# Norms that take shift and scale as sums in PSUM, with their weights loaded earlier and the split parts written directly

## What is computed

```python
mod = jax.nn.silu(c) @ ada_w[i] + ada_b[i]                  # 6 x 1024 values
sh_a, sc_a, g_a, sh_f, sc_f, g_f = jnp.split(mod[:, None, :], 6, axis=-1)
h = rms_norm(x, attn_norm[i]) * (1.0 + sc_a) + sh_a
x = x + g_a * mixer(h)
h = rms_norm(x, ffn_norm[i]) * (1.0 + sc_f) + sh_f
x = x + g_f * swiglu(h)
```

## Time and profile before

| | |
|---|---|
| median of the runs | 2864.67 us |
| profiled execution | 2865.48 us |
| its span | 2863.7 us |
| PE busy | 2196.3 us (77%) |
| PEld busy | 1930.6 us (67%) |
| DVE busy | 1775.3 us (62%) |
| ACT busy | 903.8 us (32%) |
| POOL busy | 113.3 us (4%) |
| moved by DMA | 368.84 MB, 129 GB/s on average |

### The profile page before, as it was taken

How to read it: one execution, slowest core, us unless ns; L and a number is a source line. 1 busy time by engine, 2 the same in 40 slices (tenths; PEclk the granted TensorE clock), 3 DMA queues, 4 the chain that set the end, 5 groups by cost and what they waited for, 6 DMA issues and landing times. The chain is left out here.

```text
span 2863.7 us, 43489 instructions
## 1 busy us (share of the span) xinstructions
PE 2196.3 (77%) x16766; PEld 1930.6 (67%) x16766; DVE 1775.3 (62%) x2988; ACT 903.8 (32%) x1244; POOL 113.3 (4%) x102
## 2 busy tenths in 40 slices
PE   4936665997844599679778876550679999999997
PEld 2936334996733599467476776550569999999996
DVE  2564226776775677467336668459976666666665
ACT  1300222432323233132322422220554444444443
POOL 0000000000000000043000023000000000000000
PEclk8955557999865799889765988785899999999998
DMA  5635005884702487231100000310025555555554
GB/s 184 221 59 151 0 2 183 320 310 171 258 10 76 160 299 281 74 119 59 59 3 1 5 3 27 138 59 0 0 95 185 183 189 190 184 183 190 189 183 148
DMA packets 153588, 368.84 MB, mean 129 GB/s; under 512 B 10992, under 2 KB 93680, under 8 KB 141296
## 3 DMA queue, kind: packets, MB, share of 16 engines
q1 hardware_dynamic: 153312, 365.93, 36.7%
q10 hardware_dynamic: 144, 1.05, 0.1%
HBM read 364.32 MB, written 2.62 MB: 128 GB/s over the span
## 5 line engine op out<-in xcount | busy, mean ns | idle before, releaser
L981 PE MATMUL experts_pa<-all_h_hi,experts_u_hi 128*128 128x256 f32 x1024 | 290.1, 283 | 7.4 <-DVE experts_u_lo L1052 7.4
L983 PE MATMUL experts_pa<-all_h_hi,experts_u_lo 128*128 128x256 f32 x1024 | 290.5, 284 | 0.0
L982 PE MATMUL experts_pa<-all_h_lo,experts_u_hi 128*128 128x256 f32 x1024 | 290.5, 284 | 0.0
L1228 PE MATMUL ffn_pa<-all_h_hi,ffn_u_hi 128*128 128x256 f32 x704 | 198.6, 282 | 29.6 <-DVE ffn_u_lo L1287 29.6
L1057 DVE TENSOR_TENSOR experts_v_lo<-experts_v,experts_v_hi 128x1024 fp32r<-128x1024 f32 x128 | 156.8, 1225 | 92.1 <-ACT experts_v_hi L1026 92.1
L981 PEld LDWEIGHTS experts_pa<-all_h_hi,experts_u_hi 128*128 128x128 f32 x1024 | 196.9, 192 | 12.5 <-DVE experts_u_lo L1052 7.6
L994 PE MATMUL experts_py<-experts_v_lo,experts_c_hi 128*128 128x512 f32 x512 | 201.0, 393 | 0.0
L982 PEld LDWEIGHTS experts_pa<-all_h_lo,experts_u_hi 128*128 128x128 f32 x1024 | 196.9, 192 | 4.9
L993 PE MATMUL experts_py<-experts_v_hi,experts_c_hi 128*128 128x512 f32 x512 | 200.1, 391 | 0.0
L1229 PE MATMUL ffn_pa<-all_h_lo,ffn_u_hi 128*128 128x256 f32 x704 | 198.1, 281 | 0.0
L1230 PE MATMUL ffn_pa<-all_h_hi,ffn_u_lo 128*128 128x256 f32 x704 | 197.9, 281 | 0.0
(11 more groups left out here) (543 smaller groups left out, 5467.5 us busy)
## 6 DMA issues: line engine op xcount, KB each, us to landing
experts_u<-in_peer_u SPq DMA_DIRECT2D x128, 512.0 KB, 4.4
experts_v<-in_peer_v SPq DMA_DIRECT2D x128, 512.0 KB, 3.3
ffn_u<-in_ffn_columns SPq DMA_DIRECT2D x44, 1024.0 KB, 7.9
ffn_ada_w<-in_ada_w SPq DMA_DIRECT2D x36, 1024.0 KB, 5.4
ffn_v<-in_ffn_rows SPq DMA_DIRECT2D x44, 512.0 KB, 8.1
proj_ada_w<-in_ada_w SPq DMA_DIRECT2D x12, 1024.0 KB, 5.7
proj_w<-in_diff_w_in SPq DMA_DIRECT2D x12, 1024.0 KB, 5.8
main_mod<-in_dn_w_qkv SPq DMA_DIRECT2D x24, 512.0 KB, 3.3
```

What stands on the lines that cost most here:

```text
L981: pe.matmul(out, u_hi[:, b, cols], h_hi[:, c, :], start=(c == 0), stop=False)
L982: pe.matmul(out, u_hi[:, b, cols], h_lo[:, c, :], start=False, stop=False)
L983: last = pe.matmul(out, u_lo[:, b, cols], h_hi[:, c, :], start=False, stop=(c == KT - 1))
L1228: pe.matmul(out, u_hi[:, b, cols], h_hi[:, c, :], start=(c == 0), stop=False)
```

## The change

- The stages `ada0b`, `ada1b`, `ada2b`, the two `split_h` stages and the stage that loads `ctx` are gone.
- A class `Sums` does the same sums inside other stages. For each piece of 512 columns PE does the matmul with ones and a second one, of one row, that adds the bias (loaded to one partition). Four norms (fnorm0, norm1, dnorm, dcnorm) take their scale and shift (4 pieces) directly from PSUM. The other pieces are made by PE and copied to the row by ACT in out0 (4 pieces), rope1 (8) and dnon (8).
- In `normed` the gain comes in an argument and has been loaded in an earlier stage (`constants`, ffn0, ffn1, dnout). The instructions have another order: x times the scaled gain first, and one instruction per half tile for the reciprocal and the shift.
- For norm0, fnorm0, norm1, fnorm1 and pnorm the turned h isn't copied to `h_t`: ACT writes hi from PSUM, and DVE lo. `project` and `peer_scores` then don't split h.

```diff
-def finish_modulation(nc, k, name, bias, rows):
+class Sums:
+    def __init__(self, nc, k, st, row, bias, jobs, banks):
+        self.b = st.sb("sum_b", [1, len(jobs) * CW])
+        self.psum = st.ps("sum_psum", [P, banks, CW])
...
+    def load(self, sp):
...
+            sp.dma_start(self.b[0:1, at * CW:(at + n) * CW],
+                         self.bias[self.jobs[at] * CW:(self.jobs[at] + n) * CW].unsqueeze(0)).then_inc(self.loaded, 16)
...
+    def sum(self, pe):
+        pe.wait_ge(self.loaded, self.loads)
+        for n, j in enumerate(self.jobs):
+            if n >= self.banks:
+                pe.wait_ge(self.moved, n - self.banks + 1)
+            out = self.psum[:, n % self.banks, :]
+            pe.matmul(out, self.k["ones"][:], self.row[:, j * CW:(j + 1) * CW], start=True, stop=False)
+            pe.matmul(out, self.k["ones"][0:1, :], self.b[0:1, n * CW:(n + 1) * CW], start=False, stop=True
+                      ).then_inc(self.summed, 1)
+    def move(self, act):
+        for n, j in enumerate(self.jobs):
+            act.wait_ge(self.summed, n + 1)
+            act.copy(self.row[:, j * CW:(j + 1) * CW], self.psum[:, n % self.banks, :]).then_inc(self.moved, 1)
...
-def normed(nc, k, name, x, gain, shift, scale, out_t):
+def normed(nc, k, name, x, g, shift, scale, out_t=None, row=None, loads=()):
...
+        sums = Sums(nc, k, st, row[0], row[1], [row[2] + n for n in (2, 3, 0, 1)], 4) if row else None
...
         @block.sync
         def _(sp):
-            sp.dma_start(g[:], gain.partition_broadcast(P)).then_inc(loaded, 16)
+            if sums:
+                sums.load(sp)
+            for to, of in loads:
+                sp.dma_start(to, of).then_inc(extra, 16)
+            if loads:
+                sp.wait_ge(extra, 16 * len(loads))
         @block.scalar
...
+            for n in range(4) if out_t is None else (1, 3):
                 act.wait_ge(turned, n + 1)
+                act.copy(target(k["h_hi"] if out_t is None else out_t, n), turned_tile(n)).then_inc(hi_ready, 1)
         @block.tensor
         def _(pe):
+            if sums:
+                sums.sum(pe)
             for n, (t, half) in enumerate(groups):
-                pe.wait_ge(h_ready, t + 1)
+                pe.wait_ge(h_ready, n + 1)
...
+        @block.vector
+        def _(dve):
+            done = Counted(dve, dve_done)
+            def low(n):
+                dve.wait_ge(hi_ready, n + 1)
+                dve.tensor_tensor(target(k["h_lo"], n), turned_tile(n), target(k["h_hi"], n).bitcast(F32),
+                                  ALU.subtract).then_inc(copied, 1)
+            def taken(n):
+                dve.wait_ge(turned, n + 1)
+                dve.tensor_copy(target(out_t, n), turned_tile(n)).then_inc(copied, 1)
+            def scaled_gain():
+                if sums is None:
+                    return done.at(dve.scalar_tensor_tensor(gs[:], scale, 1.0, g, ALU.add, ALU.mult))
+                for half in range(2):
+                    cols = slice(half * CW, (half + 1) * CW)
+                    dve.wait_ge(sums.summed, half + 1)
+                    at = done.at(dve.scalar_tensor_tensor(gs[:, cols], sums.psum[:, half, :], 1.0, g[:, cols], ALU.add,
+                                                          ALU.mult))
+                return at
...
+            if sums is not None:
+                mean()
+            ready = scaled_gain()
+            if sums is None:
+                mean()
+            done.wait(ready)
+            for t in range(TT):
+                weighed = done.at(dve.tensor_tensor(h[:, t, :], x[:, t, :], gs[:], ALU.mult))
+            dve.wait_ge(root_ready, 1)
+            done.wait(done.at(dve.reciprocal(ss[:], ss[:])))
+            for n, (t, half) in enumerate(groups):
+                cols = slice(half * CW, (half + 1) * CW)
+                if sums is not None:
+                    dve.wait_ge(sums.summed, 3 + half)
+                dve.scalar_tensor_tensor(h[:, t, cols], h[:, t, cols], ss[:, t:t + 1],
+                                         shift[:, cols] if sums is None else sums.psum[:, 2 + half, :], ALU.mult,
+                                         ALU.add).then_inc(h_ready, 1)
+                if out_t is None and n >= 2:
+                    low(n - 2)
+                if out_t is not None and n == 2:
+                    taken(0)
+            if out_t is None:
+                low(2)
+                low(3)
+            else:
+                taken(2)
@@ project @@
         @block.sync
         def _(sp):
+            if sums:
+                sums.load(sp)
...
         def _(pe):
-            pe.wait_ge(h_split, KT // 2)
+            if sums:
+                sums.sum(pe)
+            if h_t is not None:
+                pe.wait_ge(h_split, KT // 2)
...
             low_w(dve, 0)
+            if sums:
+                dve.wait_ge(sums.moved, len(sums.jobs))
...
-            for c in range(0, KT, 2):
+            for c in range(0, KT, 2) if h_t is not None else ():
                 act.copy(h_hi[:, c:c + 2, :], h_t[:, c:c + 2, :]).then_inc(h_hi_ready, 1)
+            if sums:
+                sums.move(act)
             high_w(0)
@@ head_norm_rope @@
         def _(act):
+            if made:
+                made.move(act)
             act.wait_ge(mean_ready, 1)
             act.activation(ss[:], ss[:], ACT.Sqrt).then_inc(root_ready, 1)
@@ swiglu, SP @@
+                if i == ring:
+                    for to, of in loads:
+                        sp.dma_start(to, of).then_inc(extra, 16)
...
-            finish_modulation(nc, k, "ada0b", ins["ada_b0"], [(mod, 4, 12)])
             project(nc, k, "out0", o_t, chunked(ins["sp_w_out"], D), residual=(x, m[2]),
+                    ada=(ins["ada_w1"], [(c, next_mod, 6 * D)], 0, 4), row=(mod, ins["ada_b0"], (4, 5, 10, 11)))
...
-                    block = nc.Block()
-                    with block as block:
-                        @block.sync
-                        def _(sp):
-                            sp.dma_start(ctx[:], ins["ctx"].rearrange("(t p) d -> p t d", p=P)).then_inc(loaded, 16)
-                            sp.wait_ge(loaded, 16)
-                    normed(nc, k, "dnorm", x, ins["norm_g2"][0], m[0], m[1], h_t[:, :, 0:S])
-                    normed(nc, k, "dcnorm", ctx, ins["norm_g2"][0], modc[:, 0:D], modc[:, D:2 * D], h_t[:, :, S:XC])
+                    g = free[:, 0:D]
+                    normed(nc, k, "dnorm", x, g, m[0], m[1], h_t[:, :, 0:S], row=(mod, ins["ada_b2"], 0),
+                           loads=[(ctx[:], ins["ctx"].rearrange("(t p) d -> p t d", p=P))])
+                    normed(nc, k, "dcnorm", ctx, g, None, None, h_t[:, :, S:XC], row=(modc, ins["ada_b2"], 0))
```

More of the change, by code:

```diff
@@ L451, in _, with project @@
                 act.copy(*source(n)).then_inc(moved, 1)
-def project(nc, k, name, h_t, chunks, residual=None, out=None, ada=None):
+def project(nc, k, name, h_t, chunks, residual=None, out=None, ada=None, row=None, loads=()):
     with Stage(nc, name) as st:
         beside = Modulation(nc, k, st, ada[0], ada[1], first=ada[2]) if ada else None
+        sums = Sums(nc, k, st, row[0], row[1], row[2], 2) if row else None
+        extra = st.sem("extra")
         halves = list(range(ada[2], ada[3])) if ada else []
@@ L571, in head_norm_rope, with _ @@
             st.sem(n) for n in ("loaded", "mean_ready", "root_ready", "dve_done"))
+        made = Sums(nc, k, st, row[0], row[1], row[2], 2) if row else None
         block = st.block()
+        if made:
+            @block.tensor
+            def _(pe):
+                made.sum(pe)
         @block.sync
         def _(sp):
+            if made:
+                made.load(sp)
             for s, (_, _, gain) in enumerate(segments):
@@ L1523, in diff_layer @@
             z = sb.sb("z", [P, TT, 3 * D])
[L1524 to L1525 removed]
+            normed(nc, k, "norm1", x, next_mod[:, 2 * D:3 * D], m[0], m[1], row=(mod, ins["ada_b1"], 0))
+            project(nc, k, "proj1", None, chunked(ins["diff_w_in"], 3 * D), out=z, ada=(*ada, 0, 6))
             zt = sb.sb("zt", [P, 16, S])
             o = sb.sb("o", [P, TT, D])
[L1528 removed]
+            head_norm_rope(nc, k, "rope1", z, [(0, 16, ins["diff_q_norm"]), (D, 16, ins["diff_k_norm"])],
+                           row=(mod, ins["ada_b1"], range(4, 12)))
             turn(nc, k, "turn1", z, [i * P for i in range(16)], zt)
@@ L2327, in delta_layer, with peer_scores @@
         h_t = st.sb("o_t", [P, KT, S])
-        head_norm(nc, k, "dnon", o, ins["dn_norm_g"], 1.0, gate=gate)
+        head_norm(nc, k, "dnon", o, ins["dn_norm_g"], 1.0, gate=gate, row=(mod, ins["ada_b2"], range(4, 12)))
         turn(nc, k, "dnot", o, [i * P for i in range(KT)], h_t)
-        project(nc, k, "dnout", h_t, chunked(ins["dn_w_out"], D), residual=(x, m[2]))
-def peer_scores(nc, k, ins, h_t, scores):
+        project(nc, k, "dnout", h_t, chunked(ins["dn_w_out"], D), residual=(x, m[2]),
```

(2 more changed lines are left out.)

143 lines of the change are left out of this document (58 added, 85 removed).

## The result

The changed kernel takes 2899.49 us (median of 4 runs, 2895.26 to 2901.2) against 2866.16 us (2864.67 to 2868.19) of the kernel before on the same chip: ratio 1.0114, 95% interval 1.0096 to 1.0131. It is slower, by 33 us; forecast were 2838 us, 27 us faster, and 2899 lies outside the range of 2822 to 2852.

What follows compares the result with a forecast made beforehand. PE was full only in the feed-forward; elsewhere each stage's own chain was taken as the bound. Terms -46.4 - 11.2 + 6.5 + 8.2 + 10.1 + 7.2 - 1.6 = -27.2 us gave 2838 us, range 2822 to 2852.

Steps and rivals of the forecast that it cites:

- Stages that go: Windows of ada0b, ada1b and ada2b with the ctx load vanish whole: -46.4 us; ctx load in dnorm put at nothing.
- Norms without sums: norm0, fnorm1 and pnorm: 11.6 us each from the stage's start, together -11.2 us.
- The one-row product at full price: In the sums on PE, a one-row matmul was taken to cost as much as one of 128 rows.
- rival 1: One-row matmuls in the sums nearly free: four pieces 5.6 us, eight 9.2; -26 us, 2812 us in all; chance 0.09.
- The chain of the sums: PE's sums inside other stages: four pieces 9.16 us, eight 16.19, the clock rising after about five slow records.
- What hangs on it: Stages with sums: four norms +6.5 us together, out0 +8.2, rope1 +10.1, dnon +7.2, the turn after dnon -1.6.
- the turn behind dnon: PE's turn after dnon meets the fast clock, so its 3.65 us halve: -1.6 us.
- norm behind its scale: fnorm0, norm1, dnorm, dcnorm wait for PE's scale pieces, done at 8.9 us; ends 17.8 or 16.9 us, +6.5 together.
- root behind the copies: In rope1 ACT copies all eight pieces before the root DVE waits for: 20.0 us against 9.91, +10.1.
- first product behind the sums: In out0 PE does four pieces before its first product, which starts at 17.4 us instead of 9.23: +8.2.
- dnon's end behind the last copy: In dnon copies follow the root and the stage ends with the last one: 19.9 us against 12.67, +7.2.
- Rival 2: Sums stay at 1.2 GHz, chains 13.8 and 27.5 us: +49 us, 2887 us in all; chance 0.08.

## Why the prediction was wrong

- **Stages that go.** Right: ada0b, ada1b and ada2b with the ctx load are gone, 46.4 us.
- **Norms without sums.** Right: 11.5, 10.9 and 11.2 us where 11.6 each was worked out. With the sums outside, all edits of the norms and the load of ctx in dnorm gave 40 us, by the experiment on the norms alone.
- **The one-row product at full price.** Right as to its own length: 0.853 us apart at the lower clock, as the records with 128 rows; rival 1 is refuted. What mattered was not the product's own length but the clock of the records beside it.
- **The chain of the sums: the failed step.** It took 9.2 and 16.2 us from ada0b and ada2b, with the words that PE "has also been idle or at 1.2 GHz, so I take the same". The rise in those rows belonged to chains of 128-row records only. In the new chains every second pair has one row; the clock stayed at 0.50 and a change of rows costs 0.29 us: 16.0 and 32.0 us, +6.8 and +15.8. PE's first sum came 1.7 to 2.3 us after the stage's start instead of 2.9 to 3.3, since the bias landed sooner, which gave back 0.6 to 1.6 of it.
- **What hangs on it.** Each stage with sums came out longer than forecast: out0 +5.6, fnorm0 +6.0, norm1 +5.9, dnorm +5.6, dcnorm +5.1, rope1 +15.3, dnon +15.2, and the turn behind dnon kept its 3.64 us, +1.6: 60.3 together. The logic of each stage (norm behind its scale, root behind the copies, first product behind the sums, dnon's end behind the last copy) was right, with DVE's idle time ended by ACT and PE as said. -27.2 + 60.3 = +33.1 us; the spans differ by 35.5 (2899.2 against 2863.7). Beside that, the three norms without sums are 1.1 us shorter than forecast, ffn0 is 1.3 longer (201.65 us against 200.34), and norm0 starts 1.1 later (50.80 against 49.67). The rest wanders in stages that the change doesn't touch: the experts' loop has 736.4 us against 733.1 before, and 732.6 to 736.3 in the eight experiments, so some 3 us of any difference here need not be the edit's.
- **Rival 2** had this mechanism, for 2887 us and a chance of 0.08. It was short by 12: it used 13.8 and 27.5 us, which are the chains measured with one row only (13.65 and 27.3), and did not have the price of the changes, 5 x 2.35 + 2 x 4.7 = 21 us, less some 9 us of earlier bias. What I set against it, that "the same matmuls with ones rose within five records each time", was no evidence: they were not the same matmuls once a one-row one stood in between. The row that bore on it was the sparse attention, full of small tiles and at 1.2 GHz; it was no proof either, since PE is busy for only 99 of the 155 us from 270 to 425.

Shown are that the one-row products cost the clock (128 rows in all against one row in all, same order and count), the price of a change (2.00 us a pair in the changed kernel against 1.71 in these two runs), the price of the place of the copies, and that the norms gain 40 us. Open is what mixture raises the clock or keeps it up, and whether the gaps at the changes of rows have a part in it: the run with the one-row records behind the others has fewer of them too. A version that has the bias in the row from the start of its accumulation, and so needs no adds either, was not tried.

## What to carry to other kernels

Price a chain on PE by rows whose tile sizes are in the same mixture, and ask of every small matmul what it does to the clock of the large ones beside it: here adding a bias with a one-row product cost more than the product's own time. Put such products behind a block of full ones or, better, add the small term elsewhere; the same results then took 2847 and 2819 us in place of 2899, and 2811 with the new order on ScalarE. And a sum moved from a stage of its own into another is only hidden where that stage's own work is longer than the whole chain, and where nothing it needs is queued behind the chain's copies.

## What the runs showed of the hardware

- PE busy for 27.00 of 27.00 us with one-row matmuls is granted 0.50 all the time; the same number of records with 128 rows has 1.00 after 2.9 to 5.6 us in the seven chains. The Trainium skill, "TensorE: Matmul & The Clock Gate", section "What's actually happening", has the clock follow how busy PE has been. If busy is what the profile counts as busy, which PE is all the time in both, this trace does not agree.
- Going from 128 rows to one or back costs about 0.29 us at the lower level and 0.19 at the upper; going from one 128-row stationary to another costs nothing (0.853 and 0.43 us a record).
- Products that nobody reads, ahead of the chain, made the kernel 29 us faster.
- A bias load into 128 partitions (two of 512 KB, 4.2 to 4.8 us from issue to landing, or one of 2048 KB, 6.8 and 7.0 us) let PE start 3.3 to 5.0 us later than the same values into one partition.
- A one-partition add of 512 columns takes 0.67 us on VectorE and 1.26 on GpSimd. Beside a long product of VectorE with two inputs it takes 3.30, and the product 3.24 in place of 2.29.
